# Earlier scaled and masked values, and the convolution moved to later slots, in a two-layer hybrid decoder kernel

## The reference

```python
# A: mLSTM, per head; w_s scales keys and values on their way into the state
w_s = jnp.exp(g_last - m_new[..., None])
C_new = dec[..., None, None] * C + jnp.einsum('bhs,bshk,bshv->bhkv', w_s, kc, vc)
n_new = dec[..., None] * n + jnp.einsum('bhs,bshk->bhk', w_s, kc)
# B: retention
S_new = chunk_dec * S + jnp.einsum('hs,bshk,bshv->bhkv', to_end, kc, vc)
# C: gated linear recurrence
S_new = jnp.exp(BL)[..., None] * S + jnp.einsum('bshk,bshv->bhkv', kc * jnp.exp(BL[:, None] - Bc), vc)
# D: short gated convolution of width 3 over time, buf holds the last 2 inputs
yconv, buf1 = _short_conv(cg_d * x_d, buf0, conv_w)
yD = bg_d * yconv
# all four
proj = jnp.einsum('btnw,nwd->btnd', jnp.stack([yA, yB, yC, yD], axis=2), w_branch)
mix = jnp.einsum('btd,de->bte', jnp.sum(gates * proj, axis=2), w_out)
```

## Time and profile before

| | |
|---|---|
| median of 3 runs | 1552.47 us (1551.88 to 1554.76) |
| profiled execution | 1555.45 us, span 1553.7 us |
| PE | 1505.2 us busy, 97% |
| PEld | 1452.0 us, 93% |
| DVE | 990.2 us, 64% |
| POOL | 962.1 us, 62% |
| ACT | 665.6 us, 43% |
| DMA | 223.36 MB, mean 144 GB/s |

### The profile page before, as it was taken

The page is one execution under the profiler, slowest core; times in us unless marked ns, Lnnn a source line. Parts: engine busy times, 40 slices in busy tenths (PEclk is TensorE's granted clock), DMA queues, the critical chain, the costliest instruction groups (busy, mean ns, idle before and its releaser), DMA issues.

```text
span 1553.7 us, 26415 instructions
## 1 busy us (share of the span) xinstructions
PE 1505.2 (97%) x10298; PEld 1452.0 (93%) x10298; DVE 990.2 (64%) x1949; ACT 665.6 (43%) x1222; POOL 962.1 (62%) x749
## 2 busy tenths in 40 slices
PE   8899999999999999999899999999999999999996
PEld 7899988998999999999899999889899999999996
DVE  3974776357876777734448747754578777777344
ACT  5534444444444544433345444434444445444333
POOL 7666545555456667777767565544545566777774
PEclk9999999999999999999999999999999999999998
DMA  8343453444544444444434335434344344444542
GB/s 283 113 134 122 142 179 113 163 129 134 169 150 162 138 136 150 150 150 150 136 110 134 120 101 198 146 125 137 124 154 165 124 153 135 149 148 142 159 149 75
DMA packets 66260, 223.36 MB, mean 144 GB/s; under 512 B 8024, under 2 KB 12632, under 8 KB 66136
## 3 DMA queue, kind: packets, MB, share of 16 engines
q1 hardware_dynamic: 66136, 221.67, 44.5%
HBM read 206.07 MB, written 15.58 MB: 143 GB/s over the span
## 4 chain that ended last, share of the span: by engine, by line
PE 88%; DVE 8%; issue 2%; ACT 2%; DMA 1%; SPq 0%; ACTq 0%; DVEq 0%
PE gps L1327 26%; PE gps L1329 25%; PE gps L1328 25%; PE xp L1563 2%; PE xp L1565 1%; PE xp L1507 1%; PE xp L1468 1%; DVE whi L870 1%; PE xp L1555 1%; PE xp L1478 1%; DVE zc L1007 1%; PE xp L1457 1%; DMA raw<-in_w 1%; PE gps L1457 1%; PE xp L1486 0%
## 5 line engine op out<-in xcount | busy, mean ns | idle before, releaser
L620 POOL TENSOR_TENSOR wlo<-raw,whi 128x512 fp32r<-128x512 f32 x724 | 946.3, 1330 | 573.0 <-ACT whi L641 341.8
L1327 PE MATMUL gps<-xh,whi 128*128 128x320 f32 (+1 forms) x2000 | 642.7, 321 | 20.4 <-DVE xl L852 7.4
L1329 PE MATMUL gps<-xh,wlo 128*128 128x320 f32 (+1 forms) x2000 | 623.8, 312 | 0.0
L1328 PE MATMUL gps<-xl,whi 128*128 128x320 f32 (+1 forms) x2000 | 623.7, 312 | 0.0
L641 ACT ACTIVATE whi<-raw 128x1024 fp32r<-128x1024 f32 x258 | 272.3, 1056 | 353.0 <-PE gps L1329 293.1
L1327 PEld LDWEIGHTS gps<-xh,whi 128*128 128x128 f32 x2000 | 380.0, 190 | 29.4 <-DVE zc L887 8.0
L1328 PEld LDWEIGHTS gps<-xl,whi 128*128 128x128 f32 x2000 | 381.8, 191 | 3.4 <-issue 0.4
L1329 PEld LDWEIGHTS gps<-xh,wlo 128*128 128x128 f32 x2000 | 380.9, 190 | 0.0
L1327 PE MATMUL gps<-ah,whi 128*128 128x320 f32 x640 | 199.2, 311 | 0.5 <-DVE al L937 0.3
L1328 PE MATMUL gps<-al,whi 128*128 128x320 f32 x640 | 197.8, 309 | 0.0
L1329 PE MATMUL gps<-ah,wlo 128*128 128x320 f32 x640 | 197.8, 309 | 0.0
(11 more groups left out here) (307 smaller groups left out, 1846.0 us busy)
## 6 DMA issues: line engine op xcount, KB each, us to landing
raw<-in_w SPq DMA_DIRECT2D x362, 512.0 KB, 3.5
s<-in_st SPq DMA_DIRECT2D x24, 512.0 KB, 4.5
out_ss<-s SPq DMA_DIRECT2D x24, 512.0 KB, 2.7
con<-in_cst SPq DMA_DIRECT2D x4, 462.0 KB, 5.0
out_sp<-pst SPq DMA_DIRECT2D x24, 64.0 KB, 2.6
mix<-in_x SPq DMA_DIRECT2D x4, 320.0 KB, 4.8
out_y<-mix SPq DMA_DIRECT2D x8, 160.0 KB, 1.9
ee<-in_cst SPq DMA_DIRECT2D x1, 224.0 KB, 3.8
```

The source lines that it names most:

```text
L620: nc.gpsimd.tensor_tensor(wlo[:, c % RING, half, :], raw[:, c % RING, half, :], whi[:, c % RING, half, :].bitcast(F32), ALU.subtract).then ...
L1327: M(out, hi, xhi, start=start, stop=False)
L1328: M(out, hi, xlo, start=False, stop=False)
L1329: return M(out, lo, xhi, start=False, stop=stop)
```

## The change

The values are made earlier. In C and B the DVE phase keeps its place in DVE's order but waits only for the state products of the head before (`("fin", -1, 0)`), not for this head's own `num` on PE. In A the five instructions move out of `a_sq` to the end of `a_score`, right behind the two that make `pt`; `numA` on PE, which waits for that phase, now waits for them too. The four convolution steps move from behind qA 3, kA 2, oA 1 and ifA to behind vB 0, vB 2, qB 2 and kB 0, where A's heads run, and get a scratch buffer of their own, as `ee` is in use there. PE's, ACT's and POOL's instructions stand in the same order as before.

```diff
-    "numC": (..., ("dve", 2)),
+    "numC": (..., ("dve", ("fin", -1, 0))),
     "numA": (("pe", (("a_score", 0, 1), ("fin", -1, 2))), ("act", 0), ("pe", ("a_score", 0, 3)), ("act", 2), ("dve", 3)),
-    "a_sq": (("act", ("num", 0, 4)), ("dve", ("num", 0, 2))),
+    "a_sq": (("act", ("num", 0, 4)),),
     "numB": (...
-             ("act", (2, ("fin", -1, 3))), ("dve", 2)),
+             ("act", (2, ("fin", -1, 3))), ("dve", ("fin", -1, 0))),
...
-    "finA": (("pe", (("a_sq", 0, 0), ("a_sq", 0, 1))), ...
+    "finA": (("pe", (("a_sq", 0, 0), ("a_score", 0, 3))), ...
...
-    beside = {index[("in", "kA", 0)] + 3 * h - 1: ("mix", "conv", "D", h) for h in range(H)}
+    beside = {index[("in", "vB", 0)] + i: ("mix", "conv", "D", h) for h, i in enumerate((0, 2, 6, 8))}
...
+        conv = sb("conv", [P, T])
...
+            def spread_values(n, h):
+
+                if n == "A":
+                    ends, mask = (ee[:, 255:256], ee[:, 383:384]), own[:, :]
+                    half = 384 + NQ * DS
+                    link(V.tensor_tensor(own[:, :], ee[0:NS, 384 + DS - 1:half:DS], ee[0:NS, half + DS - 1:SP4:DS],
+                                         ALU.add))
...
+                if ends:
+                    for i in range(2):
+                        V.tensor_scalar(vw[:, i, 0:P], v_of(n, h, i), ends[i], None, ALU.mult)
+                if n == "A":
+                    V.tensor_copy(vw[:, :, P], ee[:, 255:384:128])
+                return V.tensor_tensor(vm[:, :, :], v_of(n, h, 2).unsqueeze(1).to_broadcast([NS, NQ, P]),
+                                       mask.unsqueeze(2).to_broadcast([NS, NQ, P]), ALU.mult)
...
                 elif stage == "a_score" and k == 3:
                     V.tensor_tensor(pt[:, h, 0:384], xp[1][:, 0:384], ee[:, 0:384], ALU.mult)
-                    done(V.tensor_tensor(pt[0:NS, h, 384:SP4], xp[1][0:NS, 384:SP4], ee[0:NS, 384:SP4], ALU.mult))
+                    V.tensor_tensor(pt[0:NS, h, 384:SP4], xp[1][0:NS, 384:SP4], ee[0:NS, 384:SP4], ALU.mult)
+                    done(spread_values(n, h))
...
-                elif stage in ("num", "a_sq"):
...
+                elif stage == "num":
+                    done(spread_values(n, h))
...
-                    y = ee[:, 0:T]
+                    y = conv[:, :]
...
-                        if k == 0:
+                        if k == 0 or item[1] == "num" or (item[1], k) == ("a_score", 3):
                             settled(dve, layer, *item[1:])
```

More of the change, by code:

```diff
@@ L182 @@
     "b_score": (("pe", ("b_rope", 0, 1)), ("dve", 0)),
-    "numC": (("pe", ("fin", -1, 2)), ("act", 0), ("pe", ("fin", -1, 1)), ("act", (2, ("fin", -1, 3))), ("dve", 2)),
+    "numC": (("pe", ("fin", -1, 2)), ("act", 0), ("pe", ("fin", -1, 1)), ("act", (2, ("fin", -1, 3))), ("dve", ("fin", -1, 0))),
     "numA": (("pe", (("a_score", 0, 1), ("fin", -1, 2))), ("act", 0), ("pe", ("a_score", 0, 3)), ("act", 2), ("dve", 3)),
-    "a_sq": (("act", ("num", 0, 4)), ("dve", ("num", 0, 2))),
+    "a_sq": (("act", ("num", 0, 4)),),
     "numB": (("pe", (("b_rope", 0, 1), ("fin", -1, 2))), ("act", 0), ("pe", ("b_score", 0, 1)),
-             ("act", (2, ("fin", -1, 3))), ("dve", 2)),
+             ("act", (2, ("fin", -1, 3))), ("dve", ("fin", -1, 0))),
     "b_mean": (("pe", ("num", 0, 3)), ("dve", 0), ("act", 1)),
     "finC": (("pe", (("num", 0, 3), ("num", 0, 4))), ("dve", 0), ("act", (0, ("fin", -1, 3))), ("dve", 2)),
-    "finA": (("pe", (("a_sq", 0, 0), ("a_sq", 0, 1))), ("dve", 0), ("act", (0, ("fin", -1, 3))), ("dve", 2)),
+    "finA": (("pe", (("a_sq", 0, 0), ("a_score", 0, 3))), ("dve", 0), ("act", (0, ("fin", -1, 3))), ("dve", 2)),
     "finB": (("pe", (("b_mean", 0, 2), ("num", 0, 4))), ("dve", 0), ("act", (0, ("fin", -1, 3))), ("dve", 2)),
@@ L1000, in take @@
                 return last
+            def spread_values(n, h):
[4 more added lines that the diff above has]
+                                         ALU.add))
+                elif n == "B":
+                    toend = c_("toend")[:, 2 * h:2 * h + 2]
+                    ends, mask = (toend[:, 0:1], toend[:, 1:2]), fade[:, h, :]
+                else:
+                    ends, mask = None, same[:, :]
+                if ends:
[5 more added lines that the diff above has]
+                                       mask.unsqueeze(2).to_broadcast([NS, NQ, P]), ALU.mult)
             def phase(stage, n, h, k, layer, done):
```

## The result

The changed kernel takes 1540.72 us in the median of 4 runs (1539.37 to 1541.22), the kernel before 1552.18 in 4 runs (1551.44 to 1554.76): a ratio of 0.9917, 95% interval 0.9901 to 0.9934. On two further occasions, with more runs of before beside it, it was 0.9903 (0.989 to 0.9917) and 0.9907 (0.9893 to 0.992). The profiled execution took 1540.52 us, 14.9 less than the one of before.

A forecast was written before the change was run, and what follows sets the result against it. PE was taken as the bound. From the median 1552.47 us, 7.2 for closed gaps and 3 × 1.7 for spells gave 1540.2; with 1 us added the forecast was given as 1541.0, range 1537.5 to 1547.5.

The forecast's parts named there:

- The six gaps: PE's four waits ahead of A's state products and two for the last step of `a_gate` close: 7.2 us.
- The part at `a_gate`: PE's wait for L1039 shrinks or closes once the fourth convolution moves: 0.83 to 1.27, taken as 1.1 us a layer.
- What the moved work costs: On DVE, values and convolutions in their new places are covered by its idle time: 0, at most 1 us for values.
- SP's queue: The convolution's state write delays weights 70 and 71; ACT stands 1.7 to 2.8 us, PE has six us left: 0.
- The slower rival: Weight 70 comes too late behind SP's state write and PE waits: 1561 to 1566 us, chance 0.05.
- The clock: PE's half-clock spells of 3.4 us in the mixers' stage, 1.7 us lost each, go with the gaps: 0 to 8.5 us.
- three of the five: The median run of before was read as having about three of the profile's five half-clock spells: 3 × 1.7 us.
- the lower end: The range's fast end, 1537.5 us: all gaps closed, all spells gone and no microsecond added.
- The gaps close but the clock falls as often: Rival: PE's gaps in the mixers' stage go but its half-clock spells stay: 1545.3 us, chance 0.22.
- The wait only changes its name: Rival: PE next waits for ACT's `sq` or a late cast, half of 7.2 given back: about 1550 us, chance 0.09.
- the wait for `seen`: Sign against the prediction: a PE wait for `wlo`, `whi` or `seen` in A's heads of more than 1 us.

The follow-up runs named there:

- conv_only: The kernel before with all four convolution steps at their new places and the values made where they were; 1552.62 us, ratio 0.9984 to before.
- write_held: The changed kernel with the write of the convolution's state held until DVE has done head 2's state update; 1555.82 us, ratio 1.0002 to before.
- row_split: The changed kernel with only the last two instructions of A's row of gates moved behind the gate of C's last slot; 1541.23 us.
- fourth_only: The kernel before with only the fourth convolution step moved, behind kB 0; 1551.24 us, ratio 0.9977 to before.
- values_only: The changed kernel with the four convolution steps put back among C's heads; 1544.78 us, ratio 0.9936 to before.
- row_later: The changed kernel with the state's write issued two heads later and A's row of gates two slots later; 1551.98 us.

## Why the prediction was right, point by point

*The six gaps.* Right in place; the size was taken from the idle rows (7.2 us, by all of them 7.5) and the matmuls show 8.4. The part at `a_gate` was given as 1.1 us a layer. All 1.27 of the wait went, since L1060 ran in 0.17 us: of the two durations that the prediction weighed, the short one came.

*What the moved work costs.* Right: the values took 1.3 to 1.7 us, the convolutions 4.6 to 5.7, and PE waits for none of them. That this rests on the two halves going together was not said: the prediction priced each edit by itself, and `conv_only` shows that one of them alone opens waits of 1.61 us.

*SP's queue.* Right in mechanism: ACT's wait grew by 3.1 us, where 1.7 to 2.8 were given (at 4.87 us it is above the 2 to 3 that it was to show), and nothing on PE followed. The slower rival's threshold for the write was 326.8 for the kernel before. In the changed kernel, where slot 69 ends at 328.34, it is 322.2 by the same sum; so the changed kernel's write at 316.13 has the six us of cover that were predicted. `write_held` wrote at 322.86, and PE waited 0.88. But the rival's price was too low: by its sum (the delay past the threshold, and one or two spells of 1.7) a write 0.7 us too late costs 2.4 to 4.1 us a layer, and 7 to 8 were measured. They came from the queue behind the cast, which the sum leaves out.

*The clock.* Here a term was off. The prediction read the median run of before as holding three of the five spells, from times alone. The granted clock over the later runs speaks for all five: its mean is 0.9897 over the 49 runs of before that stood beside the experiments, and 0.9945 over 13 runs of the changed kernel. The difference of 0.0048 of some 1550 us is 7.4 us, between four and five times 1.7, and in the changed kernel that already counts spells elsewhere. The profiled execution of before, with its clock of 0.989 and five spells, was thus a usual one.

*The number.* With 8.4 for the gaps and 7.4 for the clock the gain is 15.8 less what new small waits cost, and the two later occasions measured 15.4 and 14.1. The first four runs gave 11.5. The changed kernel took the same time on all three occasions, but before was 3 us faster on the first; whether its runs held fewer spells there isn't on record. So the nearness of 1541.0 to 1540.7 is in part luck: the gaps were taken 1.2 us too small and the clock 2.3, and the start lay 2.8 us under what before took later, which makes up for most of it. The sum as written slips a little, too: 1540.2 and 1 us are 1541.2, and the lower end, with all five spells gone, is 1536.8 and not 1537.5.

*The rivals.* "The gaps close but the clock falls as often" is refuted by the clock's 0.9945. "The wait only changes its name" is true of `conv_only` and of `row_split`, and of the change only in a small part: the wait for `seen` of 1.1 to 1.3 us in two of its three profiled executions, if it comes from the change at all. By the prediction's own list this sign makes it wrong; in time it is 1 us of some 15, and the times are those of the forecast.

*What stays open.* Waits of 1.2 us and more come before each spell in the mixers' stage, but not each such wait has one. Without the waits for `seen`, `before` shows 5 spells at 8 such waits, `conv_only` 2 at 9, `fourth_only` 1 at 8, `values_only` none at 4, and the changed kernel's three profiled executions none at 2 each. After 3.5 us of waiting, in `row_later`, there was one in both layers. What decides the rest was not found.

## What to carry to other kernels

A step off the critical path still has a place in its engine's queue, and what stands behind it there is what it costs: move first what is waited for, then fill the place it had. Before a move, look at which engine works beside the new place, since an instruction may take several times as long there. And price a closed wait with the clock that goes with it, by the mean clock over many runs rather than by one profile.

## What the runs showed of the hardware

- Small DVE instructions stretch with POOL's work beside them: `capr`'s second instruction took 0.62 us with POOL idle and 1.60 beside its `wlo`, and so did parts of the convolution (0.27 and 1.32, 0.49 and 1.41 for the same shapes). These have two inputs in SBUF; with one, `capr`'s first took 0.38 and 0.83, and a copy of 2 columns 0.16 and 1.26. In `row_split` this came with a new wait of 1.42 us in place of the one of 1.26. The Trainium skill (SBUF — State Buffer, "Who interferes with whom") says that a DVE instruction with two SBUF inputs contends with a GpSimd instruction that reads SBUF, and that the ports they share are an exclusive lock. The trace agrees for the first three pairs, with up to 1.05 us more beside instructions of POOL of 1.33.
- A spell at half clock cost 1.4 to 1.6 us of its 3.4. PE's waits for the values, `a_gate` and the gates came to 1.3 us more in `conv_only` than in before (11.3 against 10.0), and it was still 0.16% faster, with a mean clock of 0.9925 against 0.9897.
- With a write of 36 KB (141 packets under 512 bytes) issued 0.4 us ahead of a 512 KB weight in the same queue, the weight was there 1.4 us later than without. This is one place in two traces; that the write is the cause wasn't tried by itself.
